# Expert retrieval on one Trainium2 core: routing head by head, with three of four chunks' key search moved behind the score loop

## The reference, cut to what matters

```
q = (x @ w_q).reshape(128, 8 heads, 2, 128)
s = einsum('chpd,hpnd->chpn', q, sub_keys)            # 16 score rows of 128 per token
st, it = lax.top_k(s, 16)                             # key search, per head and half
cand = st[:, :, 0, :, None] + st[:, :, 1, None, :]    # 256 sums per head
cidx = it[:, :, 0, :, None] * 128 + it[:, :, 1, None, :]
best, pos = lax.top_k(cand, 16);  eidx = take_along_axis(cidx, pos)
g = softmax(best)
act = gelu(einsum('chkd,cd->chk', u_tab[eidx], x))    # 128 rows of u per token
y = einsum('chk,chkd->cd', g * act, v_tab[eidx])      # 128 rows of v per token
```

## Time and profile before

| | |
|---|---|
| median of 3 runs | 2795.8 us (2783.29 to 2813.3) |
| the profiled execution, its time | 2802.86 us |
| its span, first to last instruction | 2801.0 us |
| mean granted TensorE clock | 0.904 |
| PE, DVE, POOL, ACT busy | 72%, 58%, 50%, 17% of the span |
| mean HBM rate | 287 GB/s |

### The profile page before, as it was taken

How to read it: one execution, slowest core, us unless ns; L and a number is a source line. 1 busy time by engine, 2 the same in 40 slices (tenths; PEclk the granted TensorE clock), 3 DMA queues, 4 the chain that set the end, 5 groups by cost and what they waited for, 6 DMA issues and landing times.

```text
span 2801.0 us, 19974 instructions
## 1 busy us (share of the span) xinstructions
PE 2027.4 (72%) x6119; PEld 999.7 (36%) x6119; DVE 1632.0 (58%) x3403; ACT 480.9 (17%) x1081; POOL 1402.7 (50%) x1284
## 2 busy tenths in 40 slices
PE   6788659999777977970003777767666677777998
PEld 2578534444365445440001222222222222222443
DVE  1331587977788686898898555565555544443000
ACT  0441203530033000000000111111111111112221
POOL 0000002336534561004887777767777777777552
PEclk9899779999888988985556999999999999999999
DMA  8567446569856993204998999999999999999884
GB/s 284 191 227 241 129 131 222 180 233 360 294 186 225 332 341 115 75 1 162 320 350 298 393 375 388 377 365 386 365 369 375 384 378 407 409 409 409 314 307 169
DMA packets 310373, 803.76 MB, mean 287 GB/s; under 512 B 23230, under 2 KB 142830, under 8 KB 310260
## 3 DMA queue, kind: packets, MB, share of 16 engines
q0 software_dynamic: 184320, 671.17, 64.4%
q1 hardware_dynamic: 125948, 131.31, 14.4%
HBM read 799.44 MB, written 2.94 MB: 286 GB/s over the span
## 4 chain that ended last, share of the span: by engine, by line
POOL 24%; DVE 19%; DMA 17%; PE 17%; issue 15%; PEld 3%; ACT 3%; DVEq 1%; PEldq 0%; SPq 0%; ACTq 0%; POOLq 0%
POOL big L1523 22%; DMA big<-in_peer_v_dram,eidx 10%; PE bank L599 8%; PE bank L815 4%; PEld bank L815 3%; ACT work L838 2%; DMA h_all<-in_peer_u_dram,eidx 2%; DMA ring_more<-in_peer_v_dram,eidx 2%; PE bank L583 2%; PE bank L773 1%; POOL h_all L1523 1%; DVE mix_region L1456 1%; DVE mix_region L1453 1%; DVE mix_region L1452 1%; DVE mix_region L1455 1%
## 5 line engine op out<-in xcount | busy, mean ns | idle before, releaser
L815 PE MATMUL bank<-big,work 128*128 128x512 f32 x2048 | 986.1, 616 | 540.2 <-ACT work L838 293.7
L1500 DVE CUSTOM_DVE_ANT_0 big<-big,h_all 128x1024 f32<-128x1024 f32 x512 | 617.8, 1226 | 496.2 <-DMA big<-in_peer_u_dram,eidx 494.6
L815 PEld LDWEIGHTS bank<-big,work 128*128 128x128 f32 x2048 | 366.0, 193 | 1159.7 <-issue 677.4
L1523 POOL DMA_INDIRECT big<-in_peer_u_dram,eidx x512 | 561.0, 1096 | 393.7 <-DVEq L1233 228.4
L599 PE MATMUL bank<-big 128*128 128x128 f32 (+1 forms) x2336 | 684.7, 456 | 65.1 <-DVEq L1051 33.1
L1523 POOL DMA_INDIRECT big<-in_peer_v_dram,eidx x512 | 540.0, 1055 | 205.4 <-PE bank L815 113.0
L599 PEld LDWEIGHTS bank<-big 128*128 128x128 f32 x2336 | 377.9, 204 | 359.5 <-issue 336.1
L838 ACT ACTIVATE work<-ident,gw 128x128 f32<-128x128 f32 x512 | 204.2, 401 | 1022.1 <-PE bank L815 1022.1
L1523 POOL DMA_INDIRECT h_all<-in_peer_u_dram,eidx x78 | 94.0, 1205 | 555.2 <-DVEq L1474 416.7
L1483 DVE TENSOR_TENSOR mix_region<-bank,gf_row 128x512 f32<-128x512 f32 x8 | 5.2, 686 | 221.6 <-PEq L819 221.4
L838 ACT ACTIVATE work<-bank 128x512 f32<-128x512 f32 (+2 forms) x104 | 47.6, 458 | 463.9 <-DVEq L1348 203.9
(11 more groups left out here) (180 smaller groups left out, 1464.8 us busy)
## 6 DMA issues: line engine op xcount, KB each, us to landing
big<-in_w_in_dram SPq DMA_DIRECT2D x44, 1024.0 KB, 6.9
big<-in_w_ada_dram SPq DMA_DIRECT2D x24, 1024.0 KB, 7.0
big<-in_peer_w_q_dram SPq DMA_DIRECT2D x16, 1024.0 KB, 5.5
big<-in_w_rnn_o_dram SPq DMA_DIRECT2D x8, 1024.0 KB, 8.6
big<-in_w_attn_o_dram SPq DMA_DIRECT2D x8, 1024.0 KB, 7.1
big<-in_w_out_dram SPq DMA_DIRECT2D x8, 1024.0 KB, 11.6
big<-in_peer_u_dram,eidx POOLq DMA_INDIRECT x512, 6.4
big<-in_peer_v_dram,eidx POOLq DMA_INDIRECT x512, 6.4
```

Of the source, the lines that this page charges most:

```text
L815: last = nc.tensor.matmul(psum[2 * (c % 2) + i][:, :], diag[:, (n - 1) % DIAGS, :], ring[r][:, i * 512:(i + 1) * 512], start=(k == 0), sto ...
L1500: V.tensor_tensor_reduce(ring[r], ring[r], h2_all[:, c, :], 1.0, 0.0, ALU.mult, ALU.add, dots[:, k:k + 1]).then_inc(row_used["u"], 1)
L1523: g.indirect_dma_start(dst, None, ins["peer_" + table][0], bass.IndirectOffsetOnAxis(ap=eidx[:, c, k:k + 1], axis=0)).then_inc(landed, 16)
```

## The change

- **Score loop, phase 1.** ACT now also copies every score bank to SBUF (`spread`): chunk 1's scores to one of two buffers, chunk 2's and chunks 3 and 4's to storage that is kept (`late2`, `late34`). DVE searches chunk 1 only, five operations instead of twenty, and for each head computes the ids at once (`ids`). From `hp` 2 on it also works through two u rows of chunk 1 per `hp` (`rows(EARLY_ROWS)`), 28 in all.
- **POOL** waits for ids head by head (`head_ready`) and no longer for a whole chunk. The first 36 turns use six buffers that are free during the loop (`EARLY`, `EARLY_SLOTS`); turn 36 waits until PE has left the loop (`tiles_left`). After that the ring has 18 buffers, and not 16.
- **Later chunks' search.** `route` has twelve pieces per step instead of four: eight with both key searches of a head and its sums, four with two heads' experts and ids.
- **Last step.** Of the 128 v rows of chunk 4 PE takes the even ones, DVE the odd ones (`scalar_tensor_tensor` into two accumulators, as `serve` does for chunk 0); both parts are added at the end.
- `SOFT_AT` goes from 72 to 96, and the attention tensors share one allocation, in which four of the ring buffers lie.

```diff
-    RING = 16
+    RING = 18
-    PARTS = 4
     DIAGS = 4
-    SOFT_AT = 72
+    SOFT_AT = 96
+    PIECES = PH + 4
+    EARLY_SLOTS, EARLY = 6, 36
+    EARLY_ROWS = 2
...
+        by.append("tensor" if table == "v" and (c < NCH - 1 or k % 2 == 0) else "vector")
...
+    slot_of = [n % EARLY_SLOTS for n in range(EARLY)]
+    slot_of += [(EARLY_SLOTS + n) % RING for n in range(len(turns) - EARLY)]
...
+                if ph:
+                    pe.drain().then_inc(tiles_left, 1)
...
+                def spread(hp):
+                    u = full((ph, "sc", hp))
+                    if hp >= 2:
+                        act.wait_ge(topk_done, hp - 1)
+                    run(scores_now[hp % 2], u[:, 0:P], ACT.Identity).then_inc(score_ready, 1)
+                    run(late2[:, hp, :], u[:, P:2 * P], ACT.Identity)
+                    run(late34[:, :, hp, :], u[:, 2 * P:4 * P].rearrange("p (t n) -> p t n", t=2), ACT.Identity)\
+                        .then_inc(bank_free[bank[(ph, "sc", hp)]], 1)
...
+            def rows(n):
+                for turn in range(next_turn[0], next_turn[0] + n):
+                    table, c, k = turns[turn]
+                    if by[turn] != "vector":
+                        continue
+                    r = slot_of[turn]
+                    if table == "u":
+                        dve.wait_ge(row_in[r], landings[turn])
+                        V.tensor_tensor_reduce(ring[r], ring[r], h2_all[:, c, :], 1.0, 0.0, ALU.mult, ALU.add,
+                                               dots[:, k:k + 1]).then_inc(row_used["vector"], 1)
+                    else:
+                        a_ = acc[k // 2 % 2]
+                        if k >= 4:
+                            dve.wait_ge(row_used["vector"], count_after[turn - 4])
+                        dve.wait_ge(row_in[r], landings[turn])
+                        V.scalar_tensor_tensor(a_, ring[r], gw[:, c, k:k + 1], a_, ALU.mult, ALU.add)\
+                            .then_inc(row_used["vector"], 1)
+                next_turn[0] += n
...
+            def ids(c, h0, h1):
+                S = slice(h0 * TOPK, h1 * TOPK)
+                link(V.scalar_tensor_tensor(sel[:, 0, S], sel[:, 2, S], float(NKEY), sel[:, 3, S], ALU.mult, ALU.add))
+                link(V.tensor_copy(eidx[:, c, S], sel[:, 0, S]))
+                dve.drain().then_inc(head_ready, h1 - h0)
...
+            def route(c, piece):
+                if piece < PH:
+                    for hp in (2 * piece, 2 * piece + 1):
+                        topk(c - C1, hp, late2[:, hp, :] if c == C1 + 1 else late34[:, c - C1 - 2, hp, :])
+                    best_sums(c, piece)
+                    return
+                if piece == PH:
+                    best_diffs(c)
+                h = 2 * (piece - PH)
+                experts(c, h, h + 2)
+                ids(c, h, h + 2)
+                if piece == PIECES - 1:
+                    routed(c)
...
+                    else:
+                        dve.wait_ge(score_ready, hp + 1)
+                        topk(0, hp, scores_now[hp % 2])
+                        dve.drain().then_inc(topk_done, 1)
                     if hp % 2:
                         best_sums(CH0[ph], hp // 2)
                         if hp == HP - 1:
                             best_diffs(CH0[ph])
                         experts(CH0[ph], hp // 2, hp // 2 + 1)
+                        ids(CH0[ph], hp // 2, hp // 2 + 1)
+                    if ph and hp >= 2:
+                        rows(EARLY_ROWS)
...
+                left = n_turns - (next_turn[0] - first)
+                if step[0][0] == "u" and step[0][1] + 1 < NCH:
+                    for piece in range(PIECES):
+                        route(step[0][1] + 1, piece)
+                        rows(left * (piece + 1) // PIECES - left * piece // PIECES)
...
+            pool.wait_ge(slot0_used, RING0 + 2 * SLOTS)
             for turn, (table, c, k) in enumerate(turns):
-                r = turn % RING
-                if k == 0:
-                    pool.wait_ge(route_ready, c + 1)
-                if turn >= RING:
-                    before = turns[turn - RING][0]
-                    pool.wait_ge(row_used[before], count_after[turn - RING])
+                r, before = slot_of[turn], held_before[turn]
+                if table == "u" and k % TOPK == 0:
+                    pool.wait_ge(head_ready, PH * c + k // TOPK + 1)
+                if turn == EARLY:
+                    pool.wait_ge(tiles_left, 1)
+                if before is not None:
+                    pool.wait_ge(row_used[by[before]], count_after[before])
                 fetch(table, c, k, ring[r], row_in[r])
```

More of the change, by code:

```diff
@@ L276, in hybrid_step @@
         featT = big[:, o_h + KD * N1:o_h + 2 * KD * N1].rearrange("p (k n) -> p k n", k=KD)
-        assert RING * D <= WR * TILE + 2 * KD * N1
-        ring = [big[:, r * D:(r + 1) * D] for r in range(RING)]
         mix_region = sb("mix_region", [P, KD * N1])
@@ L306, in hybrid_step @@
         diag = work[:, 0:DIAGS * P].rearrange("p (i n) -> p i n", i=DIAGS)
-        cut = wk(2)
+        cut = wk(2)[:, 0:P]
+        scores_now = [wk(2)[:, (1 + i) * P:(2 + i) * P] for i in range(2)]
         cand = wk(4, 4)
@@ L1007, in _ @@
                     act.drain().then_inc(pq_ready, 1)
+                    if ph and hp:
+                        spread(hp - 1)
+                if ph:
+                    spread(HP - 1)
                 end_stage()
@@ L1012, in diags @@
             def diags(c, k0, k1):
-                for k in range(k0, k1):
-                    n = (c - C1) * SLOTS + k
+                for turn, (table, c_, k) in enumerate(turns):
+                    if by[turn] != "tensor" or c_ != c or not k0 <= k < k1:
+                        continue
+                    n = count_after[turn] - 1
                     if n >= DIAGS:
-                        act.wait_ge(row_used["v"], n - DIAGS + 1)
+                        act.wait_ge(row_used["tensor"], n - DIAGS + 1)
                     run(diag[:, n % DIAGS, :], ident[:, :], ACT.Identity, scale=gw[:, c, k:k + 1]).then_inc(diag_ready, 1)
@@ L1478, in add_peer @@
             def add_peer(c):
-                x = x_all[:, c, :]
                 dve.wait_ge(sums_full, c - C1 + 1)
-                for i in range(2):
-                    mark(V.tensor_tensor(acc[0][:, i * 512:(i + 1) * 512], psum[2 * (c % 2) + i][:, :],
-                                         gf_row[:, 1, i * 512:(i + 1) * 512], ALU.mult))
-                chain.wait()
-                dve.drain().then_inc(sums_free, 1)
-                link(V.tensor_tensor(x, x, acc[0], ALU.add))
+                halves = [slice(i * 512, (i + 1) * 512) for i in range(2)]
@@ new lines, in add_peer @@
+                if c == NCH - 1:
+                    dve.wait_ge(row_used["vector"], count_after[-1])
+                    for i, h in enumerate(halves):
+                        link(V.tensor_tensor(acc[0][:, h], psum[2 * (c % 2) + i][:, :], acc[0][:, h], ALU.add))
+                    add_sums(c, acc)
+                else:
+                    for i, h in enumerate(halves):
+                        mark(V.tensor_tensor(acc[0][:, h], psum[2 * (c % 2) + i][:, :], gf_row[:, 1, h], ALU.mult))
+                    chain.wait()
+                    dve.drain().then_inc(sums_free, 1)
+                    link(V.tensor_tensor(x_all[:, c, :], x_all[:, c, :], acc[0], ALU.add))
@@ L1489, in _ @@
             routed(C1)
-            turn = 0
+            first = 0
             for step in steps:
-                rows = len(step) * SLOTS
-                for n in range(rows):
-                    table, c, k = turns[turn]
-                    if step[0][0] == "u" and n % (rows // PARTS) == 0 and step[0][1] + 1 < NCH:
-                        route(step[0][1] + 1, n // (rows // PARTS))
-                    if table == "u":
-                        r = turn % RING
-                        dve.wait_ge(row_in[r], 16 * (turn // RING + 1))
-                        V.tensor_tensor_reduce(ring[r], ring[r], h2_all[:, c, :], 1.0, 0.0, ALU.mult, ALU.add,
-                                               dots[:, k:k + 1]).then_inc(row_used["u"], 1)
-                    turn += 1
+                n_turns = len(step) * SLOTS
+                if step is steps[-1]:
+                    for a_ in acc:
+                        link(V.memset(a_, 0.0))
+                left = n_turns - (next_turn[0] - first)
[3 more added lines that the diff above has]
+                        rows(left * (piece + 1) // PIECES - left * piece // PIECES)
+                else:
+                    rows(left)
+                first += n_turns
```

97 lines of the change are left out of this document (53 added, 44 removed).

## The result

The changed kernel takes 2684.4 us (median of 4 runs, 2667.5 to 2687.6) against 2802.8 us of the kernel before, measured beside it (4 runs, 2783.3 to 2813.3): a ratio of 0.957, interval 0.950 to 0.964. The profiled execution took 2682.8 us, against 2802.9 before: 120 us less, where 97 had been forecast.

What follows compares the result with a forecast made beforehand. Bounds differed by stage: DVE in the score loop, POOL's fetches in steps 1 to 4, PE in the last step. Terms 57 - 16 + 57 = 98 us, 97 after small costs: 2802.9 to 2706 us, range 2657 to 2757.

Steps and rivals of the forecast that it cites:

- The last step: Chunk 4's v rows split over PE and DVE: POOL bounds at 1.28 us a row, 170 against 230, gain 57 us.
- Loop and step 1: Score loop and first step after it: less key search, 28 early rows; DVE done at 1455, not 1507, gain 52 us.
- rival B: Score loop does not shorten, as rows land late or ACT's spread holds the queries: 2736 us, chance 0.08.
- Steps 2 and 3: 32 us more DVE routing in each costs 12 us a step, less 8 us: net +16 us, bounds 0 and +40.
- the ring: Starts of steps 2 and 3: shorter pieces and the larger ring cut POOL's standing at a full ring, -8 us.
- POOL's lead: End of step 1: POOL some 12 turns ahead, not 4, but keeps about 5 us of it.
- The upper end of 0.6 us per us: Steps 2 and 3: price of DVE's other work in POOL time; 32 us more would cost 19 a step.
- Step 4: The step without routing, left at 342 us: forecast gain 0.
- Phase 0: Before the score loop: ids per head, costed with other small items at 0 to 2 us.
- A: Steps 2, 3 and last: DVE's added work locks POOL, fetches 1.62 us each; slower, 2841 us, chance 0.04.
- C: Transfers bound, not POOL: 1.38 us a fetch at 380 GB/s, last step gains 45, not 57; 2711 us, chance 0.06.
- D: Last step: PE's clock falls, 64 rows at 3.44 us are 220 us, gain 5; 2751 us, chance 0.04.

Runs made afterwards that it cites:

- set 2: Second set of experiments, on its own chip: kernel before 2802.73 us, changed kernel run again 2683.10 us, ratio 0.956; three edited kernels beside them.
- the first profile: First profiled execution of the changed kernel, 2682.8 us; the second profile is that of the unchanged rerun, 2673.2 us.
- set 1: First set of experiments, on another chip: four edits of the changed kernel; kernel before 2884.85 us, with engines halting again and again in steps 2 to 5.
- the doubled search: Changed kernel with the key search of chunks 2 to 4 done twice: 2826.98 us, ratio 0.979 to the kernel before.
- sets 1 and 3: The two sets of experiments, on other chips, where the kernel before took 2884.9 and 2885.3 us and engines halted in steps 2 to 5.

## Why the prediction was right, and the step that was off

The last step: right in size and reason. 57 us forecast, 59.8 measured; the fetches were 1.28 us apart, the last row's sum ended at 2668.56, 165 us after the step's start (170 forecast), the two more sums cost 2.4 us (2.5). Both one-edit kernels (all on PE again, and the split alone in the kernel before) say 50 to 56 us in their sets. That it stops at 1.28 us a row has two causes, level with each other and not told apart by the forecast: POOL's issue and the transfers.

Loop and step 1: right. From the loop's start they gained 57 us, with the 4 us of late start 53 on the clock, against 52; step 1 ended at 1455.4 (1455 forecast). From the first key search to the first operation of step 1 it took 132.0 us (131 forecast), and step 1 194.8 (199). One term agrees by luck. DVE was busy for 186 of 195 us, so 9 us were idle, and the forecast had 8.5, for rows that land late. But of waits for rows there is this one:

```profile
DVE ring_more L1209 <- DMA ring_more<-in_peer_u_dram,eidx: 1.2, 1, 1.2
```

The rest is in gaps of a few hundredths of a microsecond between 457 instructions. POOL kept ahead and left the step 15 turns ahead, where 12 had been forecast. That rows don't upset the order of DVE's queue (rival B) is shown by the 4.6 us of waits for rows in the loop.

Steps 2 and 3: the terms that were mis-sized. The prediction put the price of 32 us more routing a step at 12 us, between 9 and 19, and gave 8 back for the ring: -16, with 5 of POOL's lead against it: -11. Measured is +5.5, and +15.5 in the execution of set 2. The counts of fetches above give the terms. The routing made the fetches come 1.405 us apart and not 1.380, which is 13 us in the first profile, and 1.382, which is 1 us, in the second, where 24 had been forecast. The waits at a full ring fell from 10.1 to 7.1 us, 3 us where 8 had been forecast. And POOL's lead was worth 10 or 11 fetches, 14 to 15 us, where 5 had been forecast: the prediction took it that the ring fills while DVE is away and the lead is lost, but POOL stood for only 7.1 us and the 10 turns more that it had fetched in step 1 stayed fetched. So the price of the routing was put too high and the lead too low.

The upper end of 0.6 us per us is right for work in bursts: the changed kernel's work in four bursts takes 752.6 us, 33 us above the 719 before, for 58 us more of DVE's busy time (2 x 229 against 2 x 200), 0.57 per us. What the prediction priced too low is the cutting into small pieces, a gain for all of the routing, old and new. It had given only the 8 us of the full ring for it; measured are 39 to 49 us against the two profiles, 26 of them the full ring. So in bursts the added work costs 33 us, and the pieces take 39 to 49 off again. What the search alone costs in pieces is 13 us by the profiles of set 1, and not well told from chance.

Step 4: right, 1.7 us. Phase 0: the ids head by head cost more than the 0 to 2 us forecast; the loop begins 4.2 us later. Routing of chunk 0 ends at 417.6 to 421.8 us in eleven profiles with the new phase 0, and at 415.2 and 416.5 in the two with the old one. What of the rest is chance isn't settled.

The rivals: A didn't come: the mean fetch in steps 2 and 3 is 1.08 to 1.10 us, as in the kernel before, and even the doubled search lifts it by only 0.03. C's number is wrong, since step 4 takes 1.31 us a row at 405 GB/s and not 1.38. Its mechanism is nearer than the prediction held: with shorter fetches the same step stays at 1.30 us a row and the transfers bound it. D: PE stood at 0.98 of full clock (2.4 GHz) with 125 of 165 us busy. In the kernel before with the split it showed 0.87, with PE busy for 129 of 193 us.

## What to carry to other kernels

Where two engines feed each other through a ring of buffers, cut side work into pieces shorter than the ring is deep in time before pricing it; the same work cost 39 to 49 us more in four bursts than in twelve pieces (only these two sizes were run). Look for an engine that idles in one stage while it is the bound in the next, and move the next stage's work there: what the producer has fetched ahead by the stage's end isn't lost. And split the last stage, which nothing follows, over all engines that can do it. And when an engine's instruction is sometimes long, compare its end, not its length, with what its neighbour does: it may be one operand of the neighbour.

## What the runs showed of the hardware

A fetch that POOL begins while DVE is inside a row product of two SBUF operands ends 0.80 to 0.82 us after that product's end. The timeline of the changed kernel, run again, in step 3:

```profile
1817.52 1.22 DVE L1209 CUSTOM_DVE_ANT_0 big<-big,h_all 128x1024 f32<-128x1024 f32 x1
...
1817.56 1.98 POOL L1611 DMA_INDIRECT big<-in_peer_u_dram,eidx  x1 [0.31 <-issue]
...
1819.81 1.22 DVE L1209 CUSTOM_DVE_ANT_0 attn<-attn,h_all 128x1024 f32<-128x1024 f32 x1
1819.85 1.99 POOL L1611 DMA_INDIRECT big<-in_peer_v_dram,eidx  x1 [0.30 <-issue]
```

1817.52 + 1.22 = 1818.74, and the fetch ends at 1817.56 + 1.98 = 1819.54. Its next one starts 0.31 us later, just behind the start of another product, and is held again: products come 1.15 us apart, a fetch wants 1.24, so it loses each second gap and takes 2.30 us, two products. The scaled sum holds a fetch too. In the kernel before with the split:

```profile
2704.24 1.28 DVE L1521 SCALAR_TENSOR_TENSOR mix_region<-big,gw,mix_region 128x1024 f32<-128x1024 f32 x1 [2.10 <-DMA big<-in_peer_v_dram,eidx]
2704.49 1.83 POOL L1544 DMA_INDIRECT big<-in_peer_v_dram,eidx  x1 [0.31 <-issue]
```

Ends: 2705.52 and 2706.32, 0.80 us apart. But scaled sums in a row come 11.28 / 9 = 1.25 us apart, as the fetches do; those start some 0.06 us behind the start of a sum, are not held there, and stay at 0.94 us. Taking "0.94 us, or until 0.81 us after the end of the two-operand operation in which it began (for scaled sums, not within their first 0.1 us)" for each of the 1024 fetches of the latents gives the length within 0.05 us for 999 of the kernel before, 986 of the kernel after and 990 of the one with all rows on DVE; of those that took over 1 us it meets 346 of 357, 358 of 384 and 338 of 365. Most of the misses are of two kinds. A fetch that starts less than 0.04 us behind a product's start isn't held, and the product takes 1.29 us and not 1.22. The border is sharp: with few exceptions fetches up to 38 ns behind the start go free, and from 40 ns on they are held (the two above started 49 and 46 ns behind). This one, which goes free, started 39 ns behind:

```profile
1288.55 1.29 DVE L1209 CUSTOM_DVE_ANT_0 big<-big,h_all 128x1024 f32<-128x1024 f32 x1
1288.59 0.93 POOL L1611 DMA_INDIRECT big<-in_peer_u_dram,eidx  x1 [0.30 <-issue]
```

And fetches beside the routing's own operations of two SBUF operands (128x512, 0.69 us) take 1.14 to 1.36 us. With the product's second operand in PSUM, products hold no fetch: none of the 450 that began inside one took over 0.95 us. Why a scaled sum doesn't hold in its first tenth isn't shown.

The Trainium skill (SBUF — State Buffer, Who interferes with whom) says that an operation of VectorE with two SBUF inputs contends with a GpSimd instruction that reads SBUF, and one with a single SBUF input doesn't. The trace agrees in both halves if the fetch, which takes its row numbers from `eidx`, counts as such a reader: 1.98 us beside the one, 0.94 us beside the other. Its inference that descriptor generation is spared doesn't hold for these fetches, which bears out the prediction's choice of the row over the rule.

The Trainium skill (HBM Reference, Specifications) gives a core that streams alone well above its 358 GB/s share, and that share when both cores of a pair stream. The runs agree with the first: 405 to 420 GB/s where nothing halts, in all three sets. The 359 to 369 of step 4 in sets 1 and 3 is a mean over halts and not that share. Whether a neighbour was at work in them, no run here shows.
